# Two pairs of matmul operands moved 4 bytes further on in SBUF

## What is computed

```python
# first block
proj = rms_norm(x) @ w_in                      # 1024 -> 2560
x = x + mix @ w_out                            # 1024 -> 1024
q = xb @ w_query                               # 1024 -> 2048, picks 16 of 128*128 experts per head
u = expert_u[e]; act = gelu(einsum('td,thkd->thk', xb, u))
x = x + einsum('thk,thkd->td', g * act, expert_v[e])
# second block, twice
proj = x @ w_in_2                              # 1024 -> 4680
x = layer_norm(ALPHA * x + mix @ w_out_2)
```

## Time and profile before

| | |
|---|---|
| median of 3 runs | 1284.17 us (1283.83 to 1286.74) |
| the profiled execution | 1291.12 us, its span 1289.3 us |
| mean granted TensorE clock | 0.992 |
| PE, PEld busy | 97%, 93% |
| DVE, ACT, POOL busy | 55%, 53%, 50% |
| mean DMA rate | 170 GB/s |

### The profile page before, as it was taken

One profiled execution on the slowest core, in us unless ns is written; L12 is line 12 of the kernel. 1 busy time (PEld: TensorE's weight loads), 2 busy tenths in 40 slices (PEclk: granted clock), 3 DMA queues, 4 the chain that ended last, 5 costly groups with the idle time before them and its releaser, 6 DMA issues.

```text
span 1289.3 us, 26634 instructions
## 1 busy us (share of the span) xinstructions
PE 1252.8 (97%) x9857; PEld 1199.6 (93%) x9857; DVE 707.1 (55%) x1494; ACT 677.1 (53%) x1203; POOL 650.4 (50%) x285
## 2 busy tenths in 40 slices
PE   7998999999999999999999999999999999899996
PEld 5887999999989999999999999999999988699885
DVE  2453059980156667775666666666656742446424
ACT  4585444444566655555444555444564564446553
POOL 6756868888866666664000000000038666577654
PEclk9998999999999999999999999999999999899998
DMA  6735545555534444445666656666675433454432
GB/s 214 260 115 180 180 139 187 183 191 180 186 140 145 139 144 148 147 138 191 195 194 193 192 191 192 194 195 195 194 238 174 148 133 114 163 166 144 137 129 98
DMA packets 59300, 218.70 MB, mean 170 GB/s; under 512 B 6688, under 2 KB 6856, under 8 KB 58848
## 3 DMA queue, kind: packets, MB, share of 16 engines
q1 hardware_dynamic: 56592, 206.07, 48.6%
q0 software_dynamic: 1792, 8.95, 1.9%
q10 hardware_dynamic: 848, 2.75, 0.6%
HBM read 215.50 MB, written 4.21 MB: 170 GB/s over the span
## 4 chain that ended last, share of the span: by engine, by line
PE 93%; DVE 2%; POOL 2%; ACT 2%; issue 1%; DMA 0%; POOLq 0%; DVEq 0%; ACTq 0%
PE W L499 28%; PE A L499 27%; PE W L761 4%; PE A L543 4%; PE A L523 4%; PE A L550 4%; PE A L545 4%; PE A L524 4%; PE A L528 4%; POOL ringl L427 2%; PE A L663 1%; PE W L925 1%; PE A L658 1%; PE A L660 1%; PE W L577 1%
## 5 line engine op out<-in xcount | busy, mean ns | idle before, releaser
L427 POOL TENSOR_TENSOR ringl<-ring,ringh 128x1024 fp32r<-128x1024 f32 x137 | 338.0, 2486 | 151.2 <-ACT ringh L996 144.2
L457 POOL TENSOR_TENSOR ringl<-ring,ringh 128x1024 fp32r<-128x1024 f32 x126 | 302.4, 2400 | 116.7 <-ACT ringh L1154 78.7
L499 PE MATMUL W<-XTh,ringh 128*128 128x256 f32 x1024 | 292.1, 285 | 0.1
L499 PE MATMUL W<-XTl,ringh 128*128 128x256 f32 x1024 | 286.7, 280 | 0.0
L499 PE MATMUL W<-XTh,ringl 128*128 128x256 f32 x1024 | 286.6, 280 | 0.0
L499 PE MATMUL A<-Hh,ringh 128*128 128x256 f32 x1024 | 282.8, 276 | 0.0
L499 PE MATMUL A<-Hl,ringh 128*128 128x256 f32 x1024 | 282.6, 276 | 0.0
L499 PE MATMUL A<-Hh,ringl 128*128 128x256 f32 x1024 | 282.6, 276 | 0.0
L996 ACT ACTIVATE ringh<-ring 128x1024 fp32r<-128x1024 f32 x135 | 141.7, 1057 | 141.3 <-PE A L550 51.5
L1154 ACT ACTIVATE ringh<-ring 128x1024 fp32r<-128x1024 f32 x189 | 197.5, 1045 | 0.4 <-DMA ring<-exp_v 0.4
L499 PEld LDWEIGHTS W<-XTh,ringh 128*128 128x128 f32 x1024 | 195.5, 191 | 0.3 <-ACTq L1099 0.3
(11 more groups left out here) (262 smaller groups left out, 2054.0 us busy)
## 6 DMA issues: line engine op xcount, KB each, us to landing
ring<-exp_u SPq DMA_DIRECT2D x128, 512.0 KB, 3.2
ring<-exp_v SPq DMA_DIRECT2D x128, 512.0 KB, 4.2
ring<-w SPq DMA_DIRECT2D x72, 512.0 KB, 3.2
ring<-w_out SPq DMA_DIRECT2D x24, 512.0 KB, 3.2
ring<-w_in SPq DMA_DIRECT2D x20, 512.0 KB, 3.5
ring<-w_query SPq DMA_DIRECT2D x16, 512.0 KB, 3.2
skewed<-scratch POOLq DMA_DIRECT2D x1, 2048.0 KB, 11.1
H<-lng POOLq DMA_DIRECT2D x2, 1024.0 KB, 7.5
```

The lines of the kernel that those rows point to most:

```text
L427: pool.tensor_tensor(ringl[:, slot, :], ring[:, slot, :], ringh[:, slot, :].bitcast(F32), ALU.subtract)\
L457: pool.tensor_tensor(ringl[:, slot, :], ring[:, slot, :], ringh[:, slot, :].bitcast(F32), ALU.subtract)\
L499: last = pe.matmul(dst, stationary[a], moving[b], start=start and n == 0, stop=stop and n == 2, skip_group_check=True)
```

## The change

The two pairs of tiles become two tensors, and the parts are views of these that start one element (4 bytes) in. Each tensor is 8 elements (32 bytes) longer than its parts.

```diff
         home(192)
-        XTh = sb("XTh", [P, KC, T], F32R)
-        XTl = sb("XTl", [P, KC, T], F32R)
+        turned = sb("turned", [P, 2 * KC * T + 8], F32R)
+        XTh = turned[:, 1:KC * T + 1].rearrange("p (c t) -> p c t", c=KC)
+        XTl = turned[:, KC * T + 1:2 * KC * T + 1].rearrange("p (c t) -> p c t", c=KC)
         gain = sb("gain", [P, 4, KC])
...
         home(192)
-        Hh = sb("Hh", [P, 2, T], F32R)
-        Hl = sb("Hl", [P, 2, T], F32R)
+        gated_parts = sb("gated_parts", [P, 4 * T + 8], F32R)
+        Hh = gated_parts[:, 1:2 * T + 1].rearrange("p (n t) -> p n t", n=2)
+        Hl = gated_parts[:, 2 * T + 1:4 * T + 1].rearrange("p (n t) -> p n t", n=2)
```

## The result

The change makes the kernel slower: 1334.09 us (1331.06 to 1335.12, 4 runs) against 1284.0 us before (1283.38 to 1286.74), a ratio of 1.0395 with a 95% interval of 1.0378 to 1.0412. That is 50 us, outside the predicted range of 1240 to 1304.

A forecast was written before the change was run, and what follows sets the result against it. TensorE, never idle in the large stages, was taken to bound the kernel by its matmul pace. Gains of 6.9, 3.1, 1.7 and 2.3 us made 14.0, so 1284.2 - 14.0 = 1270.2 us, range 1240 to 1304.

The forecast's parts named there:

- Step 1: 256-column matmuls, moving operand 4 bytes later: best end 14.0 us gained, worst end 19.4 us lost; best end taken.
- the sign of its being wrong: The prediction is wrong if the first part of `up` stays at 178 us, or if `down` moves.
- The sum: Whole kernel: 1291.1 - 14.0 = 1277.1 us for the profiled execution; 1284.2 - 14.0 = 1270.2 us on the median.
- The forecast's own range: 256-column matmuls: most long paces become short, gain 9 to 19 us, 1265 to 1276 us, chance 0.32.
- Step 2: 912 wide matmuls, stationary operand 4 bytes later: 4.1 us either way, taken as 0.
- Step 3: ScalarE and VectorE write and read at the new address: 0.7 us at stage starts or 0, taken as 0.
- step 4: Small tensors lie 32 bytes further on, none an operand of a long stream: 0.
- What would be late next: In `up`, GpSimd (2.39 us a split) and DMA keep up with 2.72 us columns; gain or loss reaches the end time.
- Rival A: 256-column matmuls: the address of one column does not matter, paces stay; 1284 us, within 3 us; chance 0.25.
- Rival B: Mainly `down`: the new address makes the long pace hold, costing 19.4 us in all, 1303.6 us; chance 0.18.
- Rival C: All 7536 256-column matmuls: uneven start fetches a partial piece, price 3.3 to 34.3 us, total 1288 to 1298 us; chance 0.13.
- Rival D: 256-column matmuls: both paces fall to a 109.4 ns floor, 30.1 us beyond the 14.0, total 1240 us; chance 0.12.

The follow-up runs named there:

- `home(448)`: Activation parts moved to 448 modulo 512, 192 bytes above the weights' place, against the kernel before; 1283.29 us, ratio 1.0002.

## Why the prediction was wrong

**What bounds the kernel** was read rightly. TensorE has no idle time in the large stages, the pace of its matmuls is the time, and a change of pace arrived in the end time in full, as the table of stages shows. That two streams out of SBUF meet was an inference and still is; what the runs show is that the two operands' places matter together: moving the weights alone changes the pace of the moving operand's matmuls, and so does the distance with all starts even.

**Step 1, the moving operand one column later, is the step that failed**, in its sign and in its bounds. I took the two paces of the trace, 113.4 and 118.0 ns, for the ends between which any address would fall, and chose the good end because one stream had fallen from the long pace to the short one by itself. That row was about how a stream settles at one layout. It says nothing about another layout, where other paces hold: 120.07 ns in `down` and 121.8 in `up`, both outside my bounds. The expected gain of 14.0 us was a loss of about 41 us in the 256-column matmuls. The prediction had named the sign of its being wrong, a `down` that moves, and it moved by 20.4 us.

**The sum had a second fault**, which the kernel with all parts 16 bytes on lays open. There every stage has the short pace, as the forecast wanted it, and its profiled execution took 1277.8 us, near to the 1277.1 us that the sum gave for the profiled execution. But its median is 1279, not the 1270.2 us of the forecast. The 14.0 us were worked out from one execution that was 7 us above its median and then taken off the median; against the median the same change of pace was worth some 5 us. The forecast's own range, a gain of up to 19 us, also went beyond the 14.0 us that step 1 had as its best end.

**Step 2, the stationary operand of the wide matmuls**, taken at 0 with 4.1 us either way, cost about 4 us: its upper bound. Where the weights' parts, the moving operand there, are off too, the wide matmuls lose somewhat more (four take 0.94 or 0.95 us in most pieces with all parts 4 bytes on), but that is another kernel.

**Step 3 and step 4** (writers, small tensors) were right: 2 ns more for a write, all of it hidden.

**What would be late next**: nothing; the other engines simply wait longer.

**Rival A** (the address does not matter) is refuted by the change itself, and by every run but those at distance 64 with even starts. Part of what it rests on was true: at an even start at distance 64, which of the two paces a stage has is not fixed by where its operands stand. **Rival B** gave 1303.6 us for the loss of the short pace. Its place was right, `down` as the largest part, and its size too small: `down` lost 20.4 us, not 14.0, since the new pace is above the long one. **Rival C**, the uneven start, comes nearest: the loss is in every stage of the 7536 matmuls, and all parts off by 4 or by 8 bytes have it at the old distance. That a partial piece is fetched, its reason, no run shows. Its price was mis-sized. I put it between one and ten columns and took one to four, 0.44 to 1.8 ns on a matmul; measured against the 113.4 ns of an even start it is 6.7 ns in `down`, fifteen columns. **Rival D**, a floor at 109.4 ns, was seen nowhere: no run has 256-column float32r matmuls below 113.4 ns in a large stage.

The Trainium skill, SBUF — State Buffer, section Specifications (TRN2), with its cachelines of 16 bytes, spoke against the change, and the runs agree with its direction and its unit: with the distance held, 16 bytes off is free, 8 is not. Its count of one more line, as I priced it in an estimate, gave 13.3 us, where these matmuls lost about 41; one line more does not explain the size, and it says nothing of the distance. TensorE: Matmul & The Clock Gate, Part 2, Step-by-step, says that loading the next weights does not take read bandwidth from the running matmul. The runs don't bear out that the two leave each other alone: with all starts on multiples of 64 bytes, 113.4 ns at one distance are 120.1 ns at another. Whether it is read bandwidth that is lost, no record shows; that the pace depends on where both operands stand, the measurement decides.

**What stays open.** A distance of 60 with even starts cannot be built, since it is no multiple of 16, so the change's loss cannot be split between distance and start. Nor can the activations alone be off at distance 64. Shown is that uneven starts of both operands are enough at the old distance. That the activations' start does it in the change is argued: with uneven activations 56, 60 and 68 below give 119.9 to 120.1 ns in `down`, more than any of the even starts on either side, 116.7 ns at 48 and 118.9 ns at 80. What happens inside TensorE or SBUF when the streams meet isn't in any record.

## What to carry to other kernels

Where TensorE is busy without a gap, divide the time of a long stretch by its matmuls, and compare that pace between stages that do the same thing: it finds losses of 4 to 6% that no view shows as idle. In this kernel the layout of float32r operands that are streamed against freshly loaded weights had to meet two conditions, both starts on multiples of 16 bytes and the moving operand 64 bytes below the weights modulo 256; missing either in all stages cost 2 to 4% of the whole. The second is a fact of these eight distances, not a rule to carry over unmeasured. When bounding an unknown, the two values that a trace happens to show at one setting are no bounds for another setting; the range should have reached as far above the worse value as the two lay apart.

## What the runs showed that I had not expected

- The same 1512 matmuls with the same operands take 171.65 or 178.35 us, depending on the execution or on what stands elsewhere. The pace of one stage doesn't fix that of the next: after the pause the short one followed the long one in the kernel with all parts 32 bytes on (8.19 us for 72), and the long one the short one with `home(448)` (8.50 us). What picks the pace is open.
- The pace of a matmul depends on the distance between its two operands, with 16 bytes to either side of the best place costing 3.3 and 5.5 ns of 113.4, in a pattern that came back after 256 bytes and not after 128 at the one place tried (64 below and 192 above the same, 64 above 117.8 ns).
- Activations off a multiple of 16 bytes give 119.9 to 120.1 ns in `down` at the four distances tried (56, 60, 64 and 68 below), and distance 0 with even starts gives the same 120.1 ns. Whether the two faults add up isn't shown: no run has an uneven start far from distance 64.
- With only the weights' start off by 4 bytes, the pace is 118.4 to 118.5 ns in `up` and in `down` alike, with no alternation of blocks.
